# Sums of a head norm and first transposes of a pair move to score banks, and the splits at the first down granule change their order, in a two-block transformer kernel

## What is computed

```python
for l in range(DEPTH):                                   # DEPTH = 2
    f = swiglu(rmsnorm(x, ffn1_pre_g[l]), ffn1_w_gate[l], ffn1_w_up[l], ffn1_w_down[l])
    x = x + 0.5 * rmsnorm(f, ffn1_post_g[l])
    m = token_mixing(rmsnorm(x, mix_pre_g[l]), w_in[l], ...)
    x = x + rmsnorm(m, mix_post_g[l])
    f = swiglu(rmsnorm(x, ffn2_pre_g[l]), ffn2_w_gate[l], ffn2_w_up[l], ffn2_w_down[l])
    x = x + 0.5 * rmsnorm(f, ffn2_post_g[l])

def swiglu(x, w_gate, w_up, w_down):                     # d_ff = 2816
    return (jax.nn.silu(x @ w_gate) * (x @ w_up)) @ w_down
```

## Time and profile before

| | |
|---|---|
| median of three runs | 3334.01 us |
| the profiled execution | 3333.0 us |
| its span, first to last instruction | 3331.1 us |
| TensorE matmuls busy | 3278.0 us, 98% |
| DVE busy | 2002.0 us, 60% |
| ACT busy | 1499.4 us, 45% |
| POOL busy | 295.2 us, 9% |
| HBM read | 283.10 MB, 87 GB/s over the span |

### The profile page before, as it was taken

One profiled execution on the slowest core, in us unless ns is written; L12 is line 12 of the kernel. 1 busy time (PEld: TensorE's weight loads), 2 busy tenths in 40 slices (PEclk: granted clock), 3 DMA queues, 4 the chain that ended last, 5 costly groups with the idle time before them and its releaser, 6 DMA issues.

```text
span 3331.1 us, 56193 instructions
## 1 busy us (share of the span) xinstructions
PE 3278.0 (98%) x22486; PEld 2944.8 (88%) x22486; DVE 2002.0 (60%) x2730; ACT 1499.4 (45%) x2560; POOL 295.2 (9%) x161
## 2 busy tenths in 40 slices
PE   8999999999999999999999999999999999999999
PEld 7888877889889887876889889889999998899998
DVE  6664556676727664556666627746665277476643
ACT  5334445543435333446543435475443354754432
POOL 1000022100010000122100012210000022100000
PEclk9999999999999999999999999999999999999999
DMA  3334311233332332321233332112222321222222
GB/s 117 99 100 133 108 57 58 70 91 99 97 98 89 101 101 92 105 58 57 70 95 101 98 101 74 52 54 83 92 91 92 99 71 48 66 78 91 88 92 86
DMA packets 330743, 287.56 MB, mean 86 GB/s; under 512 B 9697, under 2 KB 326201, under 8 KB 330581
## 3 DMA queue, kind: packets, MB, share of 16 engines
q1 hardware_dynamic: 328569, 281.02, 27.9%
q10 hardware_dynamic: 2012, 4.24, 0.3%
HBM read 283.10 MB, written 5.27 MB: 87 GB/s over the span
## 4 chain that ended last, share of the span: by engine, by line
PE 92%; DVE 3%; ACT 3%; DMA 1%; issue 1%; SPq 0%; ACTq 0%; DVEq 0%
PE ps L657 19%; PE ps L658 18%; PE ps L659 18%; PE ps L710 7%; PE ps L708 7%; PE ps L709 7%; PE ps L763 2%; PE ps L2192 2%; PE ps L2194 2%; PE ps L2193 2%; PE ps L1806 1%; PE ps L1763 1%; PE ps L767 1%; PE ps L1790 1%; PE ps L2242 1%
## 5 line engine op out<-in xcount | busy, mean ns | idle before, releaser
L645 DVE TENSOR_TENSOR wlo<-raw,whi 128x1024 fp32r<-128x1024 f32 x340 | 407.4, 1198 | 788.9 <-ACT whi L638 785.4
L657 PE MATMUL ps<-xhi,whi 128*128 128x512 f32 (+2 forms) x2512 | 837.0, 333 | 0.0
L658 PE MATMUL ps<-xlo,whi 128*128 128x512 f32 (+2 forms) x2512 | 827.8, 330 | 0.0
L659 PE MATMUL ps<-xhi,wlo 128*128 128x512 f32 (+2 forms) x2512 | 825.0, 328 | 0.0
L638 ACT ACTIVATE whi<-raw 128x1024 fp32r<-128x1024 f32 (+1 forms) x421 | 434.7, 1035 | 666.5 <-PE ps L659 570.8
L657 PEld LDWEIGHTS ps<-xhi,whi 128*128 128x128 f32 x2512 | 473.0, 188 | 61.4 <-issue 19.2
L659 PEld LDWEIGHTS ps<-xhi,wlo 128*128 128x128 f32 x2512 | 472.5, 188 | 44.8
L658 PEld LDWEIGHTS ps<-xlo,whi 128*128 128x128 f32 x2512 | 473.4, 188 | 40.2 <-issue 0.5
L657 PE MATMUL ps<-hhi,whi 128*128 128x512 f32 (+2 forms) x1056 | 359.2, 340 | 4.9 <-issue 4.9
L658 PE MATMUL ps<-hlo,whi 128*128 128x512 f32 (+2 forms) x1056 | 358.1, 339 | 0.0
L659 PE MATMUL ps<-hhi,wlo 128*128 128x512 f32 (+2 forms) x1056 | 357.7, 339 | 0.0
(11 more groups left out here) (327 smaller groups left out, 6990.7 us busy)
## 6 DMA issues: line engine op xcount, KB each, us to landing
raw<-in_ffn_w_up_dram SPq DMA_DIRECT2D x176, 512.0 KB, 3.6
raw<-in_ffn_w_down_dram SPq DMA_DIRECT2D x120, 512.0 KB, 3.4
raw<-in_w_in_dram SPq DMA_DIRECT2D x94, 512.0 KB, 3.7
raw<-in_ffn_w_gate_dram SPq DMA_DIRECT2D x88, 512.0 KB, 3.7
raw<-in_w_out_dram SPq DMA_DIRECT2D x32, 512.0 KB, 3.3
raw<-in_ffn_w_down_dram SPq DMA_DIRECT2D x24, 256.0 KB, 2.7
tbias_scratch<-rev_scratch ACTq DMA_DIRECT2D x1, 3072.0 KB
y<-tbias_scratch SPq DMA_DIRECT2D x6, 512.0 KB, 4.6
```

The source lines that it names most:

```text
L645: eng.tensor_tensor(lo[:, 0:n], raw[slot][:, 0:n], hi[:, 0:n].bitcast(F32), ALU.subtract).then_inc(b.s.weights_split, 1)
L657: pe.matmul(o, wh, hi[:, t0:t0 + w], start=first, stop=False)
L658: pe.matmul(o, wh, lo[:, t0:t0 + w], start=False, stop=False)
L659: ins = pe.matmul(o, wl, hi[:, t0:t0 + w], start=False, stop=last)
```

## The change

Feed-forward: ACT makes the high parts of hidden tiles 2 to 5 ahead of the last silu, splits the first down granule right behind the silu, and makes tiles 6 and 7 behind that; DVE's low parts follow the same order. Mixer: both halves of the transposes of a pair's first unit go to the score bank of unit u+1 (columns 0 and 256) where no B pair is near; the norm's sums go to banks 6 and 7 and stand behind the first part of the fill, with semaphores of their own (`b_summed`, `b_logged`); in step 30 ACT copies the outputs of pair 6 ahead of the sigmoids, and DVE takes them in step 30 in place of 31.

```diff
-BESIDE_LAST = 8
-DEFER1 = (27, 30)
+BEFORE_SILU, BESIDE_LAST = 6, 8
+DEFER1 = (27,)
...
 act_ffn:
                 blocks_hi(LAST, 3, STRASSEN_GRAN)
+                for k in range(2, BEFORE_SILU):
+                    hidden_hi(k)
                 silu(LAST)
-                for k in range(2, BESIDE_LAST):
+                hi_split(LAST + 1, 0)
+                for k in range(BEFORE_SILU, BESIDE_LAST):
                     hidden_hi(k)
-                hi_split(LAST + 1, 0)
                 corner(LAST)
...
 dve_ffn:
             gate(LAST)
-            for k in range(2, BESIDE_LAST):
+            for k in range(2, BEFORE_SILU):
                 hidden_lo(k)
             lo_split(LAST + 1, 0)
+            for k in range(BEFORE_SILU, BESIDE_LAST):
+                hidden_lo(k)
             lo_split(LAST + 1, 1)
...
         def tbank(u, h):
-            return 4 + 2 * ((u + 1) % 2) if h == 1 and apart(u) else 2
+            return 4 + 2 * ((u + 1) % 2) if apart(u) and (h == 1 or u % 4 == 0) else 2
+        def tcol(u, h):
+            return SEQ // 2 if h == 1 and apart(u) and u % 4 == 0 else 0
...
 scores(u):
+                if u == B_NORM + 1:
+                    pe.wait_ge(s.b_logged, l * 2 + 2)
...
 ptrans(u, h):
-                if h == 1 and apart(u):
+                if tbank(u, h) != 2:
                     pe.wait_ge(s.scores_free, U + min(u + 2, UNITS1) + CR)
...
 norm_sums(c):
-                pe.wait_ge(s.transposed_out, TE + TEV1["x", c] + 1)
-                ins = pe.matmul(ps[:, 2, :], bd[:, :], m1.sqb[:, c, :], start=True, stop=True)
-                ins.then_inc(s.transposed, 1)
+                pe.wait_ge(s.scores_free, U + B_NORM - 1 + 1 + CR)
+                pe.wait_ge(s.transposed_out, TE + TEV1["p", B_NORM - 2, 1] + 2)
+                pe.matmul(ps[:, 6 + c, :], bd[:, :], m1.sqb[:, c, :], start=True, stop=True).then_inc(s.b_summed, 1)
...
 pe_mix1, the steps:
                     fill(st.parts[0])
+                if st.norm:
+                    norm_sums(0)
+                    norm_sums(1)
...
-                if st.extra is not None:
-                    norm_sums(0)
                 if st.vt is not None:
                     vtrans(st.vt)
                 if st.sc != 0:
                     fill(st.parts[2])
-                if st.extra is not None:
-                    norm_sums(1)
...
 act_mix1, transposed(v, h):
-                act.wait_ge(s.transposed, TE + TEV1["p", v, h] + 1)
+                act.wait_ge(s.transposed, TE + TEV1["p", v, 1 if tbank(v, 0) == tbank(v, 1) != 2 else h] + 1)
...
 act_mix1, the steps, behind the copies of the transposes:
+                if n_step == 30:
+                    for p_ in st.pairs:
+                        outputs(p_)
...
-                for p_ in st.pairs:
-                    outputs(p_)
+                if n_step != 30:
+                    for p_ in st.pairs:
+                        outputs(p_)
```

More of the change, by code:

```diff
@@ L110, in __init__ @@
         self.vt = self.sc = None
-        self.extra = None
+        self.norm = False
         self.tiles, self.tr = [], []
@@ L185, in schedule1 @@
         st.done = [g for part in st.done_in for g in part]
-    steps[B_NORM].extra = "norm"
+    steps[B_NORM].norm = True
     return steps
@@ L197, in t_events1 @@
             order.append(("v", st.vt))
-        if st.extra is not None:
-            order += [("x", 0), ("x", 1)]
     return {e: n for n, e in enumerate(order)}
@@ L535, in first_semaphores @@
             s.b_act_steps = sem(f"{b}_b_act_steps")
+            s.b_summed = sem(f"{b}_b_summed")
+            s.b_logged = sem(f"{b}_b_logged")
             s.b_scaled = sem(f"{b}_b_scaled")
@@ L1789, in ptrans @@
                 for t in range(j + 1):
-                    ins = pe.transpose(ps[:, tbank(u, h), P * t:P * t + P], m1.w[u % 3][:, h, P * t:P * t + P],
+                    c0 = tcol(u, h) + P * t
+                    ins = pe.transpose(ps[:, tbank(u, h), c0:c0 + P], m1.w[u % 3][:, h, P * t:P * t + P],
                                        ident[:, :])
@@ L1887, in transposed @@
                 act.activation(m1.pt[v % 2][:, h, :, :].rearrange("p a b -> p (a b)")[:, 0:nn],
-                               ps[:, tbank(v, h), 0:nn], ACT.Copy).then_inc(s.transposed_out, 1)
+                               ps[:, tbank(v, h), tcol(v, h):tcol(v, h) + nn], ACT.Copy).then_inc(s.transposed_out, 1)
             def exps(u):
@@ L1951, in act_mix1 @@
                         hi_split(g + 2)
-                if st.extra is not None:
+                if st.norm:
                     for c in range(2):
-                        act.wait_ge(s.transposed, TE + TEV1["x", c] + 1)
-                        act.activation(m1.rb[:, c, :], ps[:, 2, :], ACT.Ln, bias=eps[:, :],
-                                       scale=1.0 / 64).then_inc(s.transposed_out, 1)
-                    act.wait_ge(s.transposed_out, TE + TEV1["x", 1] + 2)
+                        act.wait_ge(s.b_summed, l * 2 + c + 1)
+                        act.activation(m1.rb[:, c, :], ps[:, 6 + c, :], ACT.Ln, bias=eps[:, :],
+                                       scale=1.0 / 64).then_inc(s.b_logged, 1)
+                    act.wait_ge(s.b_logged, l * 2 + 2)
                     act.activation(m1.rb[:, :, :], m1.rb[:, :, :], ACT.Exp, scale=-0.5).then_inc(s.b_act_steps, 1)
```

## The result

Five runs of the changed kernel took 3316.06 us in the median (3314.06 to 3317.84), beside 3334.01 for five of the kernel before (3331.09 to 3338.74): ratio 0.9948, interval 0.9937 to 0.9959. A second set, beside 21 runs of before, gave 3316.02 against 3332.10, ratio 0.9951 (0.9937 to 0.9964). The change saves some 16 us, 0.5%. The forecast was 3318.9, with a range of 3315.5 to 3326.0.

What follows compares the result with a forecast made beforehand. TensorE, busy 3278.0 of 3331.1 us, bounds the kernel, so only removed stops pay: 5.5 + 3.3 + 2.0 + 1.5 + 2.75 = 15.1 us. Forecast 3318.9 us, range 3315.5 to 3326.0.

Steps and rivals of the forecast that it cites:

- The 0.15 that was added to an idle time: TensorE's stops: a wait costs more than its printed idle time, 1.54 us for 1.39, so 0.15 us is added elsewhere.
- Feed-forward: First down matmul in four stages: the stop for DVE's late L645 goes whole, 1.38 us each, 5.5 us in all.
- rival A: Feed-forward: the "issue" stop is the start of new code, not the split; 3324.4 us, chance 0.10.
- Unit 0: First transposes of a pair: the wait for V's copy goes in both layers, 1.54 + 1.73 = 3.3 us.
- Norm and unit 24: Wait for second Ln goes, 2.0 us; at unit 24 sigmoids replace V's copy as the wait, 0.76 twice, 1.5 us.
- Unit 28 and the mixer's end: Stops at unit 28 and its product with V go, DVE's chain takes part back; 1.35 to 1.4 twice, 2.75 us.
- gains 0.75 of the 0.93: Mixer's end: unit 30's first DVE operation, behind a later L645, keeps 0.75 us of unit 28's 0.93.
- Rival B: Mixer: DVE's chain takes gains back as waits for L2032, leaving about 1.5 of 4.8 us; 3325.5 us, chance 0.10.
- Rival D: Every stage: a denser TensorE is granted less clock, slower if the mean is below 0.993; 3345 us at 0.990, chance 0.02.
- Rival C: Both rival A and Rival B, or the splits' new order makes its own stop; 3331 to 3334 us, chance 0.07.

Runs made afterwards that it cites:

- e1: Only the feed-forward's new order of copies and split, on the kernel before; 3326.25 us, ratio 0.9986.
- e9: Changed kernel with the sigmoids of unit 25 ahead of ACT's high half of the granule in step 25; 3314.05 us, ratio 0.9946.
- e8: Changed kernel with one w_out tile moved from step 29 to 32 and granule 25's low half moved from DVE to POOL; 3321.11 us, ratio 0.9970.
- e11_best: Changed kernel, unit 25's sigmoids first, V copied mid-units 13 and 17, DVE making granules 24/25 low halves in steps 27/29, one w_out tile moved to step 32; 3311.16 us.
- e3_norm: Only the norm's sums in banks 6 and 7 behind the first fill, on the kernel before; 3330.06 us, ratio 0.9992.
- e6_copies_first: Kernel before with only hidden_hi of tiles 2 to 5 ahead of the silu, split still behind the last two copies; 3326.64 us, ratio 0.9982.

## Why the prediction was right

**What bounds.** TensorE at 98% made each stop worth its length start to start, and no term of the forecast is off by more than 0.2 us at a place. The 0.15 that was added to an idle time is a little too small: the gain is 0.18 more than the idle time at both unit 0 stops (1.57 and 1.76 for 1.39 and 1.58), 0.19 more at unit 28, 0.20 at the norm and 0.22 at the feed-forward.

**Feed-forward.** Shown by e1, and the chance of 0.10 for rival A was the price of the name "issue". The size was 1.38 a stage for a measured 1.44. What the forecast did not see is that its two moves were each enough.

**Unit 0.** The whole stop is gone in both layers, as forecast; no wait of DVE's took its place.

**Norm and unit 24.** Net 1.07 for 1.02, and 0.67 for 0.76 with a stop left. The prediction lets both Ln run 2.5 us earlier; on the scale of before the first runs 1.4 earlier and the second 2.8, and since only the second was waited for, this changed nothing. The sigmoids were named as what is late next; e9 shows it.

**Unit 28 and the mixer's end.** This is the term with the largest miss, 1.54 for 1.35 to 1.4 a layer. The step that was mis-sized is that unit 30's first operation "gains 0.75 of the 0.93": it starts at 596.57. TensorE was 7.82 us ahead of before behind unit 24, so this is 604.39 on before's scale, and the whole 0.93 is gained. The prediction took 0.7 to 0.8 us for L2080 and the full 1.22 for L645; from start to start they take 0.60 and 1.13, since neighbouring instructions of DVE overlap a little. So L645 ends with ACT's sigmoids (596.66 and 596.52) and pushes nothing. The stops left, 0.25 and 1.38, are those forecast (0.3 and 1.4).

**The sum.** 15.1 forecast, 15.7 measured at the places. The absolute time was missed by 2.8 us, and most of that is the base: the median of three runs shown was 3334.0, that of 31 later ones 3331.7. The range had no allowance for this: 3316.06 lies only 0.6 above its lower end, two of the five runs lie below it, so that the time fell inside the range is in part luck; that the mechanism was right is not. Rival B's condition, waits for this line of more than 4 us, was not met (3.3). Rival D did not come: the mean clock is 0.999 with the change, 0.998 before. Rival C falls with A and B.

## What to carry to other kernels

Read a stop from start to start of the matmuls, name the one instruction that ends last, and then the next one behind it: the second is what is left of the stop (the sigmoids at unit 24, DVE's chain at the end). Work that only has to be done sometime goes into idle time ahead of a wait, but one of two ways to remove the same stop is enough. Before giving work to an idle engine, look at how long the instructions of the other engines take beside it, in the trace that is already there.

## What the runs showed of the hardware

**DVE beside POOL.** e8's loss had been in the trace all along, in both kernels. In the changed kernel, DVE's two scans of 384 columns of unit 26, and POOL:

```profile
578.46 3.87 DVE L2040 TENSOR_TENSOR_SCAN m_scan<-m_w,ones 128x384 f32<-128x384 f32 x2
...
578.00 2.65 POOL L645 TENSOR_TENSOR wlo<-raw,whi 128x1024 fp32r<-128x1024 f32 x1 [6.15 <-ACT whi L638]
```

In e11_best, where POOL doesn't run there, the same two:

```profile
578.40 1.81 DVE L2047 TENSOR_TENSOR_SCAN m_scan<-m_w,ones 128x384 f32<-128x384 f32 x2
```

3.87 against 1.81: 2.06 us lost to one POOL instruction of 2.65. POOL ends at 580.65, and the pair of scans 1.68 after it, nearly their full length: DVE stood still, it did not run slower. In e8 it was the same with L2043 (1.09 of its 1.23 left when POOL ended), and there POOL's L645 had itself started 0.7 inside a running scan: the scan took 1.19 us, POOL 2.87, where POOL takes 2.39 for this shape with no such neighbour. The starts are not a sure guide to who comes first: DVE's L2037 of 0.41 us, from 578.01 on, has its usual length though POOL's record starts at 578.00. The Trainium skill, "SBUF — State Buffer", section "Who interferes with whom", says that a DVE instruction with two SBUF inputs contends with a GpSimd instruction that reads SBUF. The same section calls the contention for the shared port pair an exclusive lock, and says that the order of issue decides who blocks. The trace agrees, for the scan too.

**The clock.** The 31 runs of before, grouped by the mean granted clock of the core: 3330.0 us at 0.999 (12 runs), 3332.4 at 0.998 (12), 3334.6 at 0.997 (4), 3338.7 at 0.996 (3). What differs between two profiles is short stretches at the lower level, 3.4 to 10.3 us long, which cost 1.6 us in e3_norm and 2.8 in the profile of before. They come and go from run to run of one kernel. The last 15 us aside, where every profile has such stretches, half of the 14 profiles have one at the start, beginning between 20.4 and 22.6 us, and three have one in the middle: e3_norm at 1406.1, e8_pool_fill at 1583.7, e6_copies_first at 2856.6. Each of these ten begins behind or during a stop of TensorE: at the start one of 2.2 to 2.8 us from 18.3 to 18.8 us on, in the middle 1.57 us at 1403.18, 1.75 at 1580.75, and 0.89 and 0.58 from 2854.52 on. But the other seven profiles have the same stop at the start and no such stretch, so a stop is not all that it takes, and what decides stays open. So effects under 2 us were read from places, and medians of 4 or 5 runs only where they agree with these.
